# A hybrid decoder layer on one core: key pages multiplied on VectorE too, two loads reordered, and the stick-breaking chain moved by one slot

## What is computed

```python
def compress(rows, w1, w2, pe):          # blocks of 32 rows, every 16 rows
    blk = rows[:, idx] + pe[:, None, :]
    ...
    return jax.nn.gelu(blk @ w1) @ w2

def sb_attend(q, q_pos, k, v, k_pos):
    z = jnp.einsum('bthd,bshd->bhts', q, k).astype(jnp.float32) * HEAD_DIM ** -0.5
    mask = k_pos[None, :] < q_pos[:, None]
    log_1m = jnp.where(mask, jax.nn.log_sigmoid(-z), 0.0)
    suffix = lax.cumsum(log_1m, axis=3, reverse=True) - log_1m
    a = jnp.where(mask, jnp.exp(jax.nn.log_sigmoid(z) + suffix), 0.0)
    return jnp.einsum('bhts,bshd->bthd', a.astype(v.dtype), v)
```

## Time and profile before

| | us |
|---|---|
| median of 3 runs (lowest, highest) | 2608.1 (2602.7, 2609.49) |
| the profiled execution's own time | 2617.39 |
| its span in the profile | 2615.8 |
| PE busy | 2303.3 (88%) |
| PEld busy | 1758.7 (67%) |
| DVE busy | 1229.1 (47%) |
| ACT busy | 811.3 (31%) |
| POOL busy | 619.7 (24%) |

### The profile page before, as it was taken

One profiled execution on the slowest core, in us unless ns is written; L12 is line 12 of the kernel. 1 busy time (PEld: TensorE's weight loads), 2 busy tenths in 40 slices (PEclk: granted clock), 3 DMA queues, 4 the chain that ended last, 5 costly groups with the idle time before them and its releaser, 6 DMA issues. The chain is left out here.

```text
span 2615.8 us, 42372 instructions
## 1 busy us (share of the span) xinstructions
PE 2303.3 (88%) x12990; PEld 1758.7 (67%) x12990; DVE 1229.1 (47%) x1968; ACT 811.3 (31%) x1464; POOL 619.7 (24%) x643
## 2 busy tenths in 40 slices
PE   8899993799997728888899999697999999999998
PEld 2444441655553426667677777576999999999998
DVE  1778784333333215667655666664111111135553
ACT  2122211333330004555545555422111111123332
POOL 0998984222201511221222121000000000000000
PEclk9999996799998868989978898898999999999999
DMA  7688877988861486544554363222211111122110
GB/s 249 201 260 267 265 250 224 141 119 110 109 117 31 89 207 170 145 121 121 157 130 122 102 167 104 90 81 68 74 46 47 48 44 48 44 73 73 62 45 25
DMA packets 266555, 316.94 MB, mean 121 GB/s; under 512 B 59450, under 2 KB 174564, under 8 KB 266044
## 3 DMA queue, kind: packets, MB, share of 16 engines
q1 hardware_dynamic: 205724, 244.10, 33.8%
q0 software_dynamic: 16288, 43.31, 9.5%
q10 hardware_dynamic: 44368, 27.40, 3.6%
HBM read 283.00 MB, written 36.44 MB: 122 GB/s over the span
## 5 line engine op out<-in xcount | busy, mean ns | idle before, releaser
L234 POOL TENSOR_TENSOR key_products<-key_pages,sb_q_rows 128x512 f32<-128x512 f32 x256 | 341.5, 1376 | 83.4 <-DMA key_pages<-in_cache_sb_kv 59.9
L382 PE MATMUL pp<-w_in_sb,xT_sb 128*128 128x512 f32 (+3 forms) x864 | 355.1, 571 | 6.4 <-DMA w_in_sb<-in_w_in 6.4
L2010 PE MATMUL pg<-h_turned_hi,w_gu_hi 128*128 128x344 f32 x1056 | 338.3, 320 | 9.8 <-DVE h_turned_lo L2058 9.8
L2012 PE MATMUL pg<-h_turned_hi,w_gu_lo 128*128 128x344 f32 x1056 | 338.2, 320 | 0.0
L2011 PE MATMUL pg<-h_turned_lo,w_gu_hi 128*128 128x344 f32 x1056 | 338.0, 320 | 0.0
L382 PEld LDWEIGHTS pp<-w_in_sb,xT_sb 128*128 128x128 f32 (+1 forms) x864 | 156.5, 183 | 195.8 <-issue 188.5
L659 PE MATMUL ph_c<-rows_turned,w_cmp 128*128 128x510 f32 (+1 forms) x576 | 252.0, 564 | 15.5 <-ACT rows_turned L683 12.1
L2053 DVE TENSOR_TENSOR w_gu_lo<-late,w_gu_hi 128x512 fp32r<-128x512 f32 x88 | 60.9, 692 | 402.1 <-ACT w_gu_hi L2023 402.1
L942 POOL TENSOR_SCALAR late<-late 128x128 f32<-128x128 f32 (+3 forms) x64 | 105.3, 1646 | 559.1 <-DVE late L1204 559.1
L2121 POOL DMA_DIRECT2D out_y_prompt<-y_rows x32 | 17.5, 546 | 904.9 <-DVE y_rows L2179 904.9
L2139 PE MATMUL py<-w_down_hi,act_hi 128*128 128x256 f32 x704 | 202.6, 288 | 16.6 <-DVE w_down_lo L2196 16.6
(11 more groups left out here) (286 smaller groups left out, 4195.6 us busy)
## 6 DMA issues: line engine op xcount, KB each, us to landing
key_pages<-in_cache_sb_kv SPq DMA_DIRECT2D x256, 256.0 KB, 3.1
late<-in_cache_sb_kv SPq DMA_DIRECT2D x256, 256.0 KB, 3.0
late<-in_w_gate_up SPq DMA_DIRECT2D x88, 256.0 KB, 2.9
late<-in_cache_nsa_kv SPq DMA_DIRECT2D x128, 128.0 KB, 6.1
late<-in_cache_nsa_kv POOLq DMA_DIRECT2D x128, 128.0 KB, 5.5
late<-in_w_down SPq DMA_DIRECT2D x4, 2816.0 KB, 10.6
w_in_sb<-in_w_in SPq DMA_DIRECT2D x5, 2048.0 KB, 17.6
scratch_T_hi<-turned_hi ACTq DMA_DIRECT2D x8, 896.0 KB
```

The source lines that it names most:

```text
L234: eng.tensor_tensor(prod[:, m % PR], kr[:, m % KR], qb[:, b % 2], ALU.mult).then_inc(multiplied, 1)
L382: mm = eng.matmul(pp[0:R, m % 4, 0:b - a], xT[:, u, k, 0:R], w[:, k, a:b], start=(k == 0), stop=(k == KT - 1))
L2010: eng.matmul(pg[:, e, c, 0:CW], w_hi[:, h, j, :], hT_hi[:, k, cols], start=k == 0, stop=False)
L2012: mm = eng.matmul(pg[:, e, c, 0:CW], w_lo[:, h, j, :], hT_hi[:, k, cols], start=False, stop=k == KT - 1)
```

## The change

Four parts. In the projection every eighth page (m % 8 == 7) is multiplied by VectorE itself, directly before it reduces it; products now count on two semaphores, and SyncE waits for both. In compression the six weight loads go from SyncE to ScalarE's queue, and the bias matmuls with the two copies of VectorE that belong to them go behind the prompt's transposes in `first()`. At the start of attention the masks' loads go ahead of the query rows, VectorE's casts ahead of its memsets, and GpSimd holds the second head's loads until the first six loads have landed. In the loop the chain of stick-breaking is moved by one slot: ScalarE does Abs and Exp in slot 0, Ln in slot 1, and `stick_exp` in slot 3 of the same group; VectorE does `scan` in slot 2 and the subtraction, now a function `difference`, in slot 3, in both slots at the place of the old `scan`.

```diff
+        on_vector = lambda m: m % 8 == 7
+        def wait_multiplied(eng, count):
+            if count >= 8:
+                eng.wait_ge(multiplied_v, count // 8)
+            eng.wait_ge(multiplied, count - count // 8)
...
                     if m >= KR:
-                        eng.wait_ge(multiplied, m - KR + 1)
+                        wait_multiplied(eng, m - KR + 1)
...
                 def multiply(m):
+                    if on_vector(m):
+                        return
...
                 def reduce(m):
                     b, p = divmod(m, NPAGE)
-                    eng.wait_ge(multiplied, m + 1)
+                    if on_vector(m):
...
+                        eng.wait_ge(k_loaded[m % KR], 16 * (m // KR) + 16)
+                        if m >= PR:
+                            eng.wait_ge(reduced, m - PR + 1)
+                        eng.tensor_tensor(prod[:, m % PR], kr[:, m % KR], qb[:, b % 2], ALU.mult).then_inc(multiplied_v, 1)
+                        eng.drain()
+                    else:
+                        eng.wait_ge(multiplied, m + 1 - (m + 1) // 8)
                     eng.tensor_reduce(zd[:, b, :, NPAGE - 1 - p], ...).then_inc(reduced, 1)
...
# compress: the six loads of pe, w1, w2 leave SyncE's list and open ScalarE's; its wait for bias_saved moves into first()
                 def first():
                     for q in range(4):
                         turn_pair(None, q)
+                    eng.wait_ge(w_loaded, 16 * 6)
+                    ... (the transposes and bias matmuls that opened TensorE's list)
+                    eng.wait_ge(bias_saved, 1)
...
# attend_prompt, SyncE: the three loads of masks, cmask, rowok move ahead of the two of q_rows
# GpSimd
                 load_head(0, 0, slice(6, 10))
+                eng.wait_ge(first_loaded, 96)
                 load_head(1, 1)
...
# ScalarE, in stick(N, s)
                         eng.activation(lg[:, 0:w], zs[s // 4 % 2][:, 0:w], ACT.Abs)
+                        eng.drain()
+                        eng.activation(lg[:, 0:w], lg[:, 0:w], ACT.Exp, scale=-1.0)
                     elif s % 4 == 1:
                         eng.drain()
-                        eng.activation(lg[:, 0:w], lg[:, 0:w], ACT.Exp, scale=-1.0)
-                    elif s % 4 == 2:
-                        eng.drain()
                         eng.activation(lg[:, 0:w], lg[:, 0:w], ACT.Ln, bias=1.0).then_inc(log_done, 1)
+                    elif s % 4 == 3:
+                        stick_exp(N, s)
...
# VectorE, in a slot, after stat, save_groups and out
+                        if s % 4 == 2:
+                            scan(N, s)
                         if s % 4 == 3:
-                            scan(N, s)
+                            difference(N, s)
```

More of the change, by code:

```diff
@@ L560, in _ @@
             def _(eng):
[L561 to L564, removed]
                 eng.dma_start(pt[:, :], io["page_table"].rearrange("b (o n) -> o (b n)", o=1)).then_inc(table_ready, 16)
@@ L597, in _ @@
             def _(eng):
[L598 to L607, removed]
                 def turn_pair(b, q):
@@ L671, in first @@
                         turn_pair(None, q)
+                    eng.wait_ge(w_loaded, 16 * 6)
+                    for kk in range(2):
+                        mm = eng.transpose(pv[:, kk * 16:kk * 16 + 16], pe[:, kk, :], ident[0:16, 0:16])
+                    mm.then_inc(pe_turned, 1)
+                    eng.wait_ge(pe_saved, 1)
+                    for kk in range(2):
+                        for m in range(16):
+                            mm = eng.matmul(ph[:, 0, kk:kk + 1], w1[:, kk, m // 8, m % 8, :], peT[:, kk, m:m + 1], start=(m == 0), stop=(m == 15))
+                    mm.then_inc(hidden_done, 1)
+                    eng.wait_ge(bias_saved, 1)
                 phases(eng, first, phase, values_product)
@@ L728, in first @@
                         save_pair(eng, None, 1, q)
+                    eng.wait_ge(pe_turned, 1)
+                    eng.tensor_copy(peT[:, :, :], pv[:, 0:32].rearrange("p (k m) -> p k m", k=2)).then_inc(pe_saved, 1)
+                    eng.wait_ge(hidden_done, 1)
+                    eng.tensor_copy(peb[:, :], ph[:, 0, 0:2]).then_inc(bias_saved, 1)
                 phases(eng, first, phase, save_values)
@@ L732, in _ @@
             def _(eng):
-                eng.wait_ge(bias_saved, 1)
+                for kk, s in enumerate("kv"):
+                    eng.dma_start(pe[:, kk, :], io[f"pe_cmp_{s}"][0].rearrange("(m r) d -> m (r d)", r=2)).then_inc(w_loaded, 16)
+                    eng.dma_start(w1[:, kk], io[f"w_cmp1_{s}"][0].rearrange("(a j p) n -> p a j n", a=2, p=P)).then_inc(w_loaded, 16)
+                    eng.dma_start(w2[:, kk], io[f"w_cmp2_{s}"][0]).then_inc(w_loaded, 16)
                 def phase(b, u, nb, nu, before):
@@ L1114, in stick_exp @@
                 def stick_exp(N, s):
-                    w, k = width(FRONT[(s - 4) % U]), N * NSTICK + s // 4 - 1
+                    w, k = width(FRONT[s - 3]), N * NSTICK + s // 4
                     eng.wait_ge(logw_ready, k + 1)
-                    if not (zero(N) and s < 8):
-                        m = back_of(s - 8)
+                    if not (zero(N) and s < 4):
+                        m = back_of(s - 7)
                         eng.wait_ge(turned, N * G + (m // U) * G + G0[m % U + 1])
@@ L1182, in _ @@
             def _(eng):
+                eng.wait_ge(masks_loaded, 48)
+                eng.tensor_copy(identb[:, :], ident[:, :])
+                eng.tensor_copy(masks[:, :, :], masksf[:, :, :])
+                eng.tensor_copy(cmask[:, :, :], cmaskf[:, :, :]).then_inc(consts_set, 1)
+                eng.memset(vx[:, :, :, :, HD:HD + 1], 1.0)
                 eng.memset(ones[:, :], 1.0)
@@ L1214, in scan, with difference @@
                     eng.tensor_tensor_scan(rev(dd), rev(lg), rev(rl), 0.0, ALU.add, ALU.add).then_inc(scan_done, 1)
+                def difference(N, s):
+                    w = width(FRONT[s - s % 4])
                     eng.drain()
```

24 lines of the change are left out of this document (7 added, 17 removed).

## The result

The changed kernel takes 2649.39 us (median of 4 runs, 2641.55 to 2654.42) against 2608.8 us for the kernel before (4 runs): a ratio of 1.0145, 95% interval 1.0092 to 1.0197. It is slower by some 38 us where 24 us less had been forecast, and lies above the range. The profiled execution took 2654.42 us, with a span of 2652.8.

What follows compares the result with a forecast made beforehand. TensorE's waits were taken as the bound, behind GpSimd's multiplication in the projection, DMA in compression and attention's start, and probabilities, stick weights and copies in the loop. 2608.1 with -8 -5 -3 -8 = -24 gives 2584 us; range 2553 to 2616.

Steps and rivals of the forecast that it cites:

- The terms for work: Projection, per tile: -2.46 us off GpSimd's chain, +0.90 for holds, +0.25 for the ring, +0.4 for the rotation.
- the sentence on SyncE: Projection: the queue behind SyncE's new wait holds next pages and the row of x, both loaded some pages ahead.
- VectorE's pages get in the way: Rival, chance 0.17: rotation pays 1.28 us, SyncE's issues hold the pace; projection +3, half the loop's gain, 2600 us.
- the bound on when the weights land: Compression: weights sharing with pages land between 457 us (served first) and 472 us (a third each).
- The share: Compression: weights sharing the DMA engines with pages get a third each at the late end, 472 us.
- Start of attention, -3 forecast: Start of attention: reordered loads and casts and holding the second head's loads save 3 us, ends 0 and -11.
- the two starts are only bytes: Rival, chance 0.12: compression and start of attention are DMA-bound, so reordering moves nothing; -16 us, 2592 us.
- the sum -26.5 + 18 = -8: Loop: 26.5 us of TensorE waits go; 12 us return at the widest tile and 6 at the other 56 scans.
- pays back more: Rival, chance 0.10: shorter stops keep TensorE at 2.4 GHz in the loop, 36 us more gained; 2548 us.
- slower, since the scan precedes the window's maximum: Rival, chance 0.13: the scan delays the window's transposes in more widths; loop loses 25 us, sum +9, 2617 us.
- the widest tile's stop becomes one longer one: Loop: argument set against the rival that the clock pays back more; no size given.
- The sign of being wrong that was set for the clock: Loop: the prediction is wrong if the granted clock moves by more than 0.03 from 0.89.

Runs made afterwards that it cites:

- e5: Only VectorE's pages put on the kernel before, with VectorE multiplying its page two reductions earlier; ratio 0.9999, last projection transposes at 430.25 us.
- e2: Only the compression part (weight loads on ScalarE's queue, bias behind the prompt's transposes) put on the kernel before; ratio 1.0034, compression 381.3 us.
- e9: Compression part alone on the kernel before, with cached pages loaded only after the six weight loads have landed; ratio 1.0015, compression 375.9 us.
- e4: Only the loop part (stick-breaking chain moved) put on the kernel before; ratio 1.0063, loop 684.6 us.
- e13: Loop part alone on the kernel before, plus 184 unread filling matmuls ahead of the window's transposes; ratio 0.9879, loop 629.1 us.
- e7: Loop part alone on the kernel before, but VectorE's scan back in slot 3 behind the window's maximum; ratio 1.0126, loop 700.4 us.
- e8: Loop part alone on the kernel before, but the scan at the head of slot 2, ahead of the selected branch's maximum; ratio 1.0026, loop 666.1 us.
- e6: Compression part alone on the kernel before, but the six weight loads back at the head of SyncE's list; ratio 0.9999, compression 374.6 us.
- e1: Only VectorE's pages, multiplied in their turn, put on the kernel before; ratio 1.0020, projection ends at 445.4 us.

## Why the prediction was wrong

**Projection, -8 forecast, +12.5.** The terms for work were no smaller than what was measured: GpSimd lost the work of 32 pages, VectorE's multiplication took 1.06 us in the mean, under the 1.13 of the earlier trace rows, and GpSimd's mean rose from 1.376 to 1.391 us only, where 0.45 us for each of VectorE's pages had been put. The step that failed is the sentence on SyncE: its new wait was costed at nothing, since "both are loaded some pages ahead". SyncE may load page m only once page m - 6 is multiplied, and VectorE multiplies a page when its list comes to it, behind a rotation or copies; all loads stand behind that, 39.9 us in 18 waits. e5 shows that the loss goes with that place. The rival "VectorE's pages get in the way" named SyncE and said +3; it priced the pace of SyncE's issues, not a stop behind a late product. The Trainium skill (SBUF — State Buffer, Who interferes with whom) was weighed for a smaller matter: VectorE's multiplication took 1.64 us at 183.70 us, where one of GpSimd's had begun 0.17 us before, and 0.68 us at 211.53 us, where none was under way, which agrees, and decided nothing.

**Compression, -5 forecast, +8.7.** The step that failed is the bound on when the weights land, 457 to 472 us. They landed at 497.3; less the 12.5 us by which the projection ended later that is 485, and e2, with the projection as before, gives 484 in the same way. The last load took 30.6 us from issue to landing, where it took 6.4 before. The share was right: I gave the weights a third of the bytes, and ScalarE's queue moved 2.18 of 6.89 MB. The rate was wrong: 472 comes out at a third of 270 GB/s, which the earlier trace rows show before the pages begin, and with pages under way all queues together moved 180 GB/s. The 13.81 us of bias matmuls then ran while the page buffers were full and the DMA engines stood still, where they had run under page loads. The Trainium skill (DMA: Bandwidth & Descriptors, Queues, rings and completion order) says that a DMA engine goes round its queues packet by packet; the shares of the three queues (38.8, 32.8 and 30.8% of the engines' time) agree in kind, and the landing is later than the late end taken from it, since the rate was lower. e9, in which pages stay out of the way, brings the weights to 463.

**Start of attention, -3 forecast, +0.1.** The rival "the two starts are only bytes" was right here: the first scores came 5.5 us earlier and the next two waits took it back.

**Loop, -8 forecast, +13.8 (16 us by e4's ratio).** The step that failed is the sum -26.5 + 18 = -8, in two places. The saving was about right: of the 26.5 us of waits 0.9 are left. What returns was put at 18 us and measured 30.4: 22.4 at the probabilities, as foreseen, and 8.0 at ScalarE's copies, which the sum did not have. So TensorE stood still 63.3 us where it had been 60.2, +3 and not -8. The other 10.8 us of the loss are no stop at all: the same 4152 matmuls took 620.5 us in place of 609.8, with the clock at 0.87 in place of 0.89. A stop has a second price, the clock of the work behind it; the sum put that at nothing, and I gave it only one sign ("pays back more", chance 0.10). e13 against e4 shows that this price is the larger one, some 70 us of TensorE's busy time in that loop, most of it there before the change as well. The rival "slower, since the scan precedes the window's maximum" named the place, its waits (16.8 to 39.2 us), and its sign. But its price was a sum of stops too, and by that a return of 30.4 us (0.48 us a group) makes a loss of some 5 us; moving the waits back (e7) did not help. That it had the sign right was in good part luck. Against the forecast's sign stood a sentence of its own: "the widest tile's stop becomes one longer one". The sign of being wrong that was set for the clock, a move of more than 0.03, did not show, with a move of 0.02: it was too wide for this loss.

Open is why about the same sum of stops goes with so different a clock in e7 and e8, and why the loop's clock differs between executions that leave it alone (0.89 to 0.92): stops were counted, and the count does not say.

## What to carry to other kernels

When work of one engine's chain moves to another, ask what else counted on its progress: a ring is refilled in order, so one product that is late in the new engine's list holds every load behind it, and the remedy here was to do that product earlier. Do not add up TensorE's stops as if a microsecond were a microsecond: compare the granted clock and the time at the lower level of two orders, and try filling the stops with work nobody reads before reordering, measuring one filling first. A load that another engine needs soon should not share its time with a long stream: e6 sent it first, e9 held the stream back, and both brought the stage back. And price such a sharing by the rate at which the stream itself runs.

## What the runs showed of the hardware

The scatter between executions of one kernel goes with the clock: 31 runs of the kernel before beside e1 to e4 have a mean granted clock from 0.921 (2623.0 and 2624.55 us) to 0.933 (2602.31 us), about 18 us for 0.01 by a straight line through all of them. With pages under way three queues moved 180 GB/s where 270 were moved before them, and shared the engines' time almost evenly. Filling matmuls that add 44 us of work to TensorE shortened a loop by 55 us. A matmul of 128 columns in 32 bits took 0.24 us there, as two instructions, twice what I had reckoned.
